# The last of eight experts as two-pass panels between those of the first two

## The reference, cut to what matters

```python
def moe_swiglu(h, w_router, w_gate_up, w_down):
    t = h.reshape(-1, D)                               # 256 x 1024
    logits = (t @ w_router).astype(F32)
    top_val, top_idx = lax.top_k(logits, TOP_K)        # 2 of 8 experts for a token
    top_w = jax.nn.softmax(top_val, axis=-1)
    combine = jnp.sum(jax.nn.one_hot(top_idx, N_EXPERTS) * top_w[..., None], axis=1)
    out = jnp.zeros_like(t)
    for e in range(N_EXPERTS):
        gt, up = jnp.split(t @ w_gate_up[e], 2, axis=-1)   # 1024 -> 2 x 3584
        y = (jax.nn.silu(gt) * up) @ w_down[e]             # 3584 -> 1024
        out = out + combine[:, e:e + 1] * y
    return out
```

## Time and profile before

| | us |
|---|---|
| median of 3 runs | 3124.39 |
| lowest, highest run | 3118.46, 3126.42 |
| span of the profiled execution | 3122.5 |
| PE busy | 3014.5 (97%) |
| DVE busy | 2007.9 (64%) |
| ACT busy | 1512.8 (48%) |
| HBM read | 602.26 MB, 193 GB/s over the span |

### The profile page before, as it was taken

One profiled execution on the slowest core, in us unless ns is written; L12 is line 12 of the kernel. 1 busy time (PEld: TensorE's weight loads), 2 busy tenths in 40 slices (PEclk: granted clock), 3 DMA queues, 4 the chain that ended last, 5 costly groups with the idle time before them and its releaser, 6 DMA issues. The chain is left out here.

```text
span 3122.5 us, 43115 instructions
## 1 busy us (share of the span) xinstructions
PE 3014.5 (97%) x17959; PEld 2637.2 (84%) x17959; DVE 2007.9 (64%) x2237; ACT 1512.8 (48%) x1692; POOL 24.1 (1%) x41
## 2 busy tenths in 40 slices
PE   7999998899999999999999999999999999999998
PEld 6889897788888899778888888998789798997898
DVE  4547647555455467498898987554555756787755
ACT  4543343334344345477777776443434445432453
POOL 0001000000000000000000000000000000000000
PEclk9999999999999999999999999999999999999999
DMA  5338650065555567599999998541445143345142
GB/s 194 132 124 265 223 185 28 9 242 189 188 189 184 173 211 243 201 361 351 354 363 350 370 349 298 174 145 60 141 167 177 42 162 135 135 152 177 55 169 95
DMA packets 197852, 606.10 MB, mean 194 GB/s; under 512 B 19648, under 2 KB 59401, under 8 KB 154394
## 3 DMA queue, kind: packets, MB, share of 16 engines
q1 hardware_dynamic: 192306, 588.23, 53.0%
q0 software_dynamic: 3872, 12.71, 1.3%
q10 hardware_dynamic: 1480, 2.41, 0.3%
HBM read 602.26 MB, written 1.05 MB: 193 GB/s over the span
## 5 line engine op out<-in xcount | busy, mean ns | idle before, releaser
L2121 DVE TENSOR_TENSOR w_lo<-ring,w_hi 128x2048 fp32r<-128x2048 f32 x336 | 769.7, 2292 | 336.2 <-ACT w_hi L2016 331.0
L2016 ACT ACTIVATE w_hi<-ring 128x2048 fp32r<-128x2048 f32 x336 | 643.1, 1915 | 367.4 <-PE ps L1963 153.4
L358 DVE TENSOR_TENSOR w_lo<-ring,w_hi 128x2048 fp32r<-128x2048 f32 (+2 forms) x209 | 469.4, 2247 | 480.1 <-ACT w_hi L349 479.4
L349 ACT ACTIVATE w_hi<-ring 128x2048 fp32r<-128x2048 f32 (+2 forms) x209 | 392.7, 1881 | 645.1 <-PE ps L470 488.4
L470 PE MATMUL ps<-h_hi,w_hi 128*128 128x256 f32 x1616 | 463.7, 287 | 17.6 <-DVE w_lo L358 10.7
L470 PE MATMUL ps<-h_lo,w_hi 128*128 128x256 f32 x1616 | 459.7, 284 | 0.0
L470 PE MATMUL ps<-h_hi,w_lo 128*128 128x256 f32 x1616 | 459.5, 284 | 0.0
L470 PEld LDWEIGHTS ps<-h_hi,w_hi 128*128 128x128 f32 x1616 | 312.5, 193 | 22.2 <-issue 17.0
L470 PEld LDWEIGHTS ps<-h_lo,w_hi 128*128 128x128 f32 x1616 | 312.6, 193 | 0.3
L470 PEld LDWEIGHTS ps<-h_hi,w_lo 128*128 128x128 f32 x1616 | 312.6, 193 | 0.0
L1926 PE MATMUL ps<-w_hi,h_hi 128*128 128x512 f32 x672 | 266.6, 397 | 1.4 <-DVE w_lo L2121 1.4
(11 more groups left out here) (539 smaller groups left out, 5544.3 us busy)
## 6 DMA issues: line engine op xcount, KB each, us to landing
ring<-in_moe_w_gate_up SPq DMA_DIRECT2D x224, 1024.0 KB, 4.9
ring<-in_moe_w_down SPq DMA_DIRECT2D x112, 1024.0 KB, 4.9
ring<-in_w_in SPq DMA_DIRECT2D x58, 1024.0 KB, 6.9
ring<-in_w_in_even SPq DMA_DIRECT2D x30, 1024.0 KB, 6.9
ring<-in_dense_w_gate_up SPq DMA_DIRECT2D x22, 1024.0 KB, 7.7
ring<-in_w_in_odd SPq DMA_DIRECT2D x16, 1024.0 KB, 6.7
arena<-in_w_ada POOLq DMA_DIRECT2D x24, 512.0 KB, 4.9
ring<-in_b_w_in SPq DMA_DIRECT2D x12, 1024.0 KB, 6.2
```

The lines of the kernel that those rows point to most:

```text
L349: k.nc.scalar.activation(self.part(k.w_hi, b, m), src, ACT.Copy).then_inc(k.hi_ready, 1)
L358: k.nc.vector.tensor_tensor(self.part(k.w_lo, b, m), src, self.part(k.w_hi, b, m).bitcast(F32), ALU.subtract).then_inc(k.lo_ready, 1)
L2016: nc.scalar.activation(high(g, h), raw(g, h), ACT.Copy).then_inc(k.hi_ready, 1)
L2121: nc.vector.tensor_tensor(low(g, h), raw(g, h), high(g, h).bitcast(F32), ALU.subtract).then_inc(k.lo_ready, 1)
```

## The change

Rank 7 (`EIGHTH`, at most 64 rows) no longer comes last. Its 14 gate panels follow panels of rank 0, its 7 down panels follow the first 7 panels of rank 1. Its rows are picked once, before the first panel, with the high parts in columns 0 to 63 and the low parts in columns 64 to 127 of one stationary tile: two passes (high weights, low weights) in place of three. `fold_rows` adds the two halves of the rows and transposes in one. For the whole ranks the hidden values now stay in one float32 copy (`hidden_whole`), and `down_parts` splits four chunks at a time, one panel ahead, into two alternating buffers. Up to rank 7's last panel there are three buffers for split halves instead of two; for the rest of rank 1 there are two again. In every `gate_up`, the passes with the high weights now come first and need only `hi_ready`. The core of the diff (changes of numbering are left out):

```diff
+FOLLOWS = {0: [0], 1: [1, 2], 5: [6, 7], **{c: [c + 1] for c in (2, 3, 4)}, **{c: [c + 2] for c in range(6, 12)}}
+def panel_order():
+    order = []
+    for c in range(PANELS):
+        order.append((0, c))
+        order += [(EIGHTH, n) for n in FOLLOWS.get(c, ())]
+    for c in range(PANELS):
+        order.append((1, c))
+        if c < DOWN_PANELS:
+            order.append((EIGHTH, GATE_PANELS + c))
+    return order + [(e, c) for e in range(WHOLE_RANKS, EIGHTH) for c in range(PANELS)]
...
+    three_until = position[EIGHTH, PANELS - 1]
...
     def buffer(g, h):
-        return 2 * ((g - TWO_TILE_RANKS * PANELS) % 2) + h if four(g) else h
+        if four(g):
+            return 2 * ((g - four_from) % 2) + h
+        if g <= three_until:
+            return (0, 1, 4)[(2 * g + h) % 3]
+        return h
...
     def buffer_free(eng, g, h):
-        back = 2 if four(g - 2) else 1
+        before = used_before(g, h)
...
+        elif before and before[1] == 0:
+            eng.wait_ge(k.first_half_used, r.pairs + before[0] + 1)
+        elif before:
+            eng.wait_ge(k.panel_used, r.first + before[0] + 1)
...
             def gate_up(e, c):
...
+                    pe.wait_ge(k.hi_ready, r.halves + 2 * g + h + 1)
...
+                            for i, xs in enumerate((x_hi,) if eighth(e) else (x_hi, x_lo)):
+                                nc.tensor.matmul(k.ps[:, u % 3, :], xs[:, 4 * h + kk, t * P:(t + 1) * P],
+                                                 w_hi[:, kk, :], start=(h == 0 and kk == 0 and i == 0), stop=False)
+                    pe.wait_ge(k.lo_ready, r.halves + 2 * g + h + 1)
...
+            def fold_rows(c):
+                pe.wait_ge(product_ready, unit(EIGHTH, c, 0) + 1)
...
+                for j in range(4):
+                    at = slice(j * EIGHTH_ROOM, (j + 1) * EIGHTH_ROOM)
+                    last = nc.tensor.matmul(k.ps[:, 4 + c % 2, at], v.eighth_sums[c % 2][:, j * P:(j + 1) * P],
+                                            v.fold, start=True, stop=True)
...
             def down(e, c):
+                if whole(e):
+                    pe.wait_ge(down_ready, e * DOWN_PANELS + c - GATE_PANELS + 1)
...
-            turn_identity(k, 96, 7)
+            turn_identity(k, 30, 7)
+            pick(EIGHTH)
+            turn_one_hot(EIGHTH)
+            turn_identity(k, 56, 7)
...
+            def down_parts(e, n):
+                if n >= 2:
+                    act.wait_ge(k.panel_used, r.first + position[e, GATE_PANELS + n - 2] + 1)
...
+                act.wait_ge(hidden_ready, e * GATE_PANELS + 2 * n + 2)
+                nc.scalar.activation(v.down_parts[n % 2][0], v.hidden_whole[:, 4 * n:4 * n + 4, :],
+                                     ACT.Copy).then_inc(down_high, 1)
...
+            for g, (e, c) in enumerate(order[0:whole_end]):
+                split(g + 1, 0)
+                if eighth(e):
...
+                    split(g + 1, 1)
+                    continue
+                if eighth_next(g):
+                    split(g + 1, 1)
...
+                    continue
+                if c < GATE_PANELS:
+                    silu(e, c)
...
+                split(g + 1, 1)
+                if 1 <= c <= GATE_PANELS:
+                    hidden_parts(e, c - 1)
...
+                if GATE_PANELS - 1 <= c < PANELS - 1:
+                    down_parts(e, c + 1 - GATE_PANELS)
...
+            def down_parts(e, n):
+                dve.wait_ge(down_high, e * DOWN_PANELS + n + 1)
+                hi, lo = v.down_parts[n % 2]
+                nc.vector.tensor_tensor(lo, v.hidden_whole[:, 4 * n:4 * n + 4, :], hi.bitcast(F32),
+                                        ALU.subtract).then_inc(down_ready, 1)
...
+            def eighth_sums(c):
+                nc.vector.tensor_copy(v.eighth_sums[c % 2], k.ps[:, unit(EIGHTH, c, 0) % 3, :]).then_inc(product_ready, 1)
...
+            mark(EIGHTH)
+            nc.vector.tensor_tensor(v.fold, k.ident[:, 0:EIGHTH_ROOM], k.ident[:, EIGHTH_ROOM:P],
+                                    ALU.add).then_inc(fold_made, 1)
...
+            pick(EIGHTH)
             for h in range(2):
                 split(0, h)
```

More of the change, by code:

```diff
@@ new lines, in gate_up @@
+                    pe.wait_ge(k.lo_ready, r.halves + 2 * g + h + 1)
+                    for t in range(n):
+                        u = unit(e, c, t)
+                        for kk in range(4):
+                            last = nc.tensor.matmul(k.ps[:, u % 3, :], x_hi[:, 4 * h + kk, t * P:(t + 1) * P],
+                                                    w_lo[:, kk, :], start=False, stop=(h == 1 and kk == 3))
+                    last.then_inc(k.first_half_used if h == 0 else k.panel_used, 1)
@@ L1936, in down @@
                 elif c == GATE_PANELS and e > 0:
-                    pe.wait_ge(added, e)
-                hidden = v.hidden_turned if turned_rank(e) else v.hidden[n]
+                    pe.wait_ge(added, added_before(e))
+                hidden = v.hidden_turned if turned_rank(e) else v.down_parts[c % 2] if whole(e) else v.hidden[n]
                 for h in range(2):
@@ L1992, in _ @@
                         turn_one_hot(e)
[L1993 to L2000, removed]
+                    for n in folds_at(g):
+                        fold_rows(n)
+                    continue
+                down(e, c)
+                if c == GATE_PANELS and turned_rank(e):
+                    turn_one_hot(e)
+                elif c == GATE_PANELS:
+                    turn_hidden(e, GATE_PANELS - 1)
+                if c == GATE_PANELS + 2 and e + 1 < EIGHTH and not whole(e + 1):
+                    pick(e + 1)
             turn_identity(k, 20, 3)
-            give_back(EXPERTS - 1)
+            give_back(EIGHTH - 1)
             turn_identity(k, 72, 3)
@@ new lines, in _ @@
+            for g, (e, c) in enumerate(order[whole_end:], whole_end):
+                todo = prepared(g)
+                for n in todo[:-1]:
+                    split(n, 0)
+                    split(n, 1)
+                if len(todo) > 1:
+                    silu(e, c)
+                if todo:
+                    split(todo[-1], 0)
+                if c < GATE_PANELS and not turned_rank(e) and len(todo) < 2:
+                    silu(e, c)
+                if c == PANELS - 1:
+                    y_parts(e)
+                if c == 0 and turned_rank(e):
+                    low_sums(e, c)
+                if todo:
+                    split(todo[-1], 1)
+                if c < GATE_PANELS and turned_rank(e):
+                    if c > 0:
+                        low_sums(e, c)
+                    silu(e, c)
+                if c == (GATE_PANELS if turned_rank(e) else 0):
+                    turned_slots(e)
+                if 1 <= c <= GATE_PANELS:
+                    hidden_parts(e, c - 1)
+                if c == GATE_PANELS + 2 and e + 1 < EIGHTH:
+                    pick(e + 1)
@@ new lines, in _ @@
+            for g, (e, c) in enumerate(order[whole_end:], whole_end):
+                todo = prepared(g)
+                for n in todo[:-1]:
+                    split(n, 0)
+                    split(n, 1)
+                if len(todo) > 1:
+                    product(e, c)
+                if todo:
+                    split(todo[-1], 0)
+                if c < GATE_PANELS and not turned_rank(e) and len(todo) < 2:
+                    product(e, c)
+                if c == PANELS - 1:
+                    y_parts(e)
+                if c == 0 and turned_rank(e):
+                    sums(e, c)
+                if todo:
+                    split(todo[-1], 1)
+                if c < GATE_PANELS and turned_rank(e):
+                    if c > 0:
+                        sums(e, c)
+                    product(e, c)
+                if c == 0 and not whole(e - 1):
+                    add(e - 1)
+                if 1 <= c <= GATE_PANELS:
+                    hidden_parts(e, c - 1)
+                if c == GATE_PANELS and e + 1 < EIGHTH:
+                    mark(e + 1)
+                if c == GATE_PANELS + 2 and e + 1 < EIGHTH:
+                    pick(e + 1)
```

402 lines of the change are left out of this document (262 added, 140 removed).

## The result

The changed kernel took **3155.62 us** (median of 4 runs, 3154.43 to 3156.67), the kernel before 3125.4 (4 runs, 3118.46 to 3130.89): a ratio of 1.0096, 95% interval 1.0084 to 1.0109. It is slower by 30 us, at 5 us from the forecast and inside its range. The profiled executions have spans of 3153.4 and 3122.5 us.

A forecast was written before the change was run, and what follows sets the result against it. TensorE's count of matmuls was taken to bound the experts. Savings of 123.8 and 3.5 us against added work, start, waits and clock summed to +26.2 on a span of 3122.5; with 1.9 for the median, 3150.6 us, range 3133 to 3168.

The forecast's parts named there:

- Removed, and the new place: Rank 7's end place and pick go, -123.8 us; its matmuls, giving back and folds among other ranks' panels add +90.6.
- Pairs: A whole gate panel plus a rank-7 gate panel with its fold takes 15.9 us, without TensorE idling.
- the folds: Rank 7's 14 gate panels each need four float32 products, 0.9 us a panel, +12.6 us in all.
- The loads don't bind: Interleaved panels need 264 GB/s, under 374 reached; the rival that loads or the alternating product bind: 3165 us, chance 0.07.
- The start, the first pair, the junction: Later first matmul +2.1 us; first whole and rank-7 pair waits +1.3; return to two buffers after rank 7 about +1.2.
- The waits: TensorE waits for down_parts before whole ranks' down panels: +34.8 us in rank 1, +9.9 in rank 0.
- The early high passes: In rank 3's first panel, high-weight matmuls run while low weights are awaited: -3.5 us; elsewhere 0.
- No wait; I put 0: Between interleaved whole and rank-7 panels, splits arrive before TensorE needs them: 0, with up to 0.3 us a pair otherwise.
- The clock: Half clock behind eight new TensorE gaps of 3.0 to 5.7 us costs 1.7 us each, +13.6; ends 0 and twice that.
- the waits are hidden: Rival: down panels' parts are ready at the preceding panel's end, so waits and clock cost vanish; 3092 us, chance 0.08.
- The clock stays up: Rival: the new down-panel waits come but bring no half clock; +12.6 us, 3137 us, chance 0.20.
- Each resumption runs longer: Rival: half clock behind each of eight down-panel gaps costs twice 1.7 us; +39.8 us, 3164 us, chance 0.15.

The follow-up runs named there:

- parts first: Changed kernel with down_parts moved before the weight splits of its step on ACT and DVE; 3093.66 us.
- filled kernel: Changed kernel with 45 identity transposes (20 and 42 in two shorter ones) run by TensorE in its eight waits; 3146.68 us.
- low half first: Changed kernel with gate and up panels, except the last rank's by count, waiting for both weight halves and interleaving the three products; 3167.48 us.
- the two reordered kernels: Changed kernel with down_parts before the splits on ACT and DVE, 3093.66 us; the same with 22 instead of 56 starting transposes, 3091.24 us.
- graded fill: Changed kernel with seven of the eight waits filled in part, by 38 down to 10 transposes; 3144.31 us.

## Why the prediction was right

The working gave +26.2 us, the stage shows +30.8. Term by term:

- **Removed, and the new place.** The last expert takes 120.1 us again, as the forecast had it. Pairs were to take 15.9 us and take 15.95; the folds, costed from a row with an eighth of their width, were 0.9 and are 0.98 (15.95 less the 11.34 and 3.63 of the forecast), 13.7 for 12.6. The page on precision (the Trainium skill, FP8 and Floating Point Precision, TensorE Precision Notes) would have made them 6; the measurement decides for the row. The loads don't bind: at 292 GB/s TensorE is full.
- **The start, the first pair, the junction.** 1.75 for 2.1 (17.72 us from the transposes to the first matmul for 15.97), 1.19 for 1.3, 0.79 for 1.2.
- **The waits.** Forecast 34.8 and 9.9, with 5.68 for most. The trace has 32.7 for rank 1's six, 1.1 more at the pick, and 8.5 before rank 0's panels 14 and 15. The five small ones of the forecast (1.2, before rank 0's panels 16 to 20) are there as well and cost 1.9: panels 16 to 19 take 11.26 us each where parts first has 10.88. Timeline of the changed kernel before panel 17, where the weight load of the first matmul waits and the matmul comes 0.47 us behind the one before it instead of 0.23:

```profile
905.13 0.39 PE L2087 MATMUL ps<-w_hi,down_lo 128*128 128x512 f32 x1
905.60 0.19 PEld L2087 LDWEIGHTS ps<-w_hi_third,down_hi 128*128 128x128 f32 x1 [0.51 <-DVE down_lo L2426]
```

Parts first gave back 61.8: these 42.3 and 1.9, the 16.6 of the clock, and 2.5 more, some 0.3 for each of these stops, less the 1.5 of the last point below. I read the 0.3 as the restart itself: idle time is counted from the modelled end of a matmul, 0.39 after its begin, while the next would follow 0.23 after it, and in the filled kernel the second matmul behind a stop comes 0.33 behind the first. With short stops and restart the waits are 46.7 for 44.7.
- **The early high passes.** From rank 2's result to rank 3's: 136.73 us before, 133.31 after, 3.4 for 3.5. But the step "No wait; I put 0" came true by luck, for a reason that it did not name: with the low half first TensorE does wait between the pairs. My arrival times were those of a single rank-7 panel with a fold; rank 1's pairs have none, and twice two rank-7 panels come in a row. The high passes cover that, about 8 us.
- **The clock.** This is the term that was mis-sized most: 8 x 1.7 = 13.6 was forecast, 16.6 measured, 2.1 a stop. The row that I used, 1.7 behind a stop of 3.87 us, lies between the 1.5 and the 2.6 seen here.
- **A term that the forecast did not have.** In rank 2's second gate panel, whose matmuls are the same in both kernels, TensorE stops for 1.51 us in both. Timeline of the kernel before, then of the changed one:

```profile
1122.73 4.11 PE L1900 MATMUL ps<-picked_both,w_hi 128*128 128x340 f32 x16 [1.51 <-DVE arena L2155]
```

```profile
1279.80 2.80 PE L1982 MATMUL ps<-picked_both,w_hi 128*128 128x340 f32 x16 [1.51 <-DVE arena L2368]
```

The granted clock behind it is 0.59 (1123 to 1127 us) in the first and 1.00 (1280 to 1284 us) in the second, and from this stop to rank 2's next of 1.28 us (1238.24 and 1393.80) they take 115.51 and 114.00 us: the changed kernel has 1.5 less. In parts first the clock falls there again (0.57 from 1219 to 1223 us).

The terms, with those for the matmuls and for giving back as forecast, sum to -123.8 + 91.7 + 1.2 + 0.8 + 1.75 + 46.7 - 3.4 + 16.6 - 1.5 = +30.1, within 1 us of the stage. The mechanism is the one forecast. That the total is off by less than 5 us owes a little to errors of both signs: clock, waits and folds came out 6.1 dearer, the fall in rank 2 and the smaller terms some 2.3 cheaper.

Of the rivals, *the waits are hidden* was wrong for this kernel and right for parts first: its 3092 us is about what the two reordered kernels take (3093.66 and 3091.24). *The clock stays up* is the filled kernel's stage (+12.6 forecast, +14.2 measured). *Each resumption runs longer* is right in direction for half of the stops. By the rule of the Trainium skill (TensorE: Matmul & The Clock Gate, What's actually happening) that the half clock is the default and activity lifts it, all eight stops would cost, and they did; but the five of the graded fill did not.

## What to carry to other kernels

When operands are made just ahead of their use, ask of each where it stands in its engine's order and what the instruction before it waits for: here DVE had time to spare, and a subtraction of 1.22 us cost TensorE 5.5 each time, because it stood behind a split that waits for the end of the very panel that it should hide under. Price a stop of TensorE with the slow matmuls behind it (here 2.1 us on 5.2), and look at the granted clock on both sides. If the work ahead of the wait can't be moved, filler on TensorE gives the clock's part back and nothing else.

## What the runs showed of the hardware

- The half clock has no fixed place: before rank 0's panel 14 it was there while TensorE still idled, and behind the stop of 3.45 us it came after about 1.4 us of full speed (an estimate from the 0.85 of the window from 1211 to 1213). Nor does the length of a stop alone tell: 2.90 (graded fill) and 2.48 (the pick, in the changed kernel) kept 1.00, while the clock fell behind 2.61 with the low half first and around 1.98 in the later attention. The same stop of 1.51 us in the same code cost 1.5 us in the kernel before and nothing in the changed one. No run here tells what decides.
- Filled waits took 16.6 us from the stage and 7.7 from the profiled span (3153.4 to 3145.7), because code that nobody edited took 6.5 us more behind the stage, with the clock at 0.50 where it is 1.00 in another kernel, and 2.4 more ahead of it. Differences under some 10 us are better read in the stage than in the total, and within the stage by the panel, as the 1.5 us of rank 2 show.
